# Row transposes of the first three tiles, of the sample tokens and of the memory keys and values: on TensorE instead of by DMA

## The chip, the cores and the metric

One Trainium2 chip, all 8 cores, each with its own eighth of the prompt streams and of the sample streams; the cores don't exchange data. The time is that of the slowest core, in microseconds of the device, as the median of several runs. One execution was profiled as well; its trace is of the slowest of its cores, core 2, unless another is named.

## The reference, cut to what matters

One layer for two groups of tokens with shared weights. Cut to shapes and order:

```
z = x @ w_in                       # 1024 -> 2560: u | v | B | C | x_in
a = u * (W_s masked @ layernorm(v) + b_s)          # per 128-token block, 4 heads
b = B * conv3(C * x_in)                            # causal, depthwise
x = layernorm(ALPHA * x + [a | b] @ w_out)
q = x @ w_q ; p = softmax(q . mem_k / 16) ; o = p @ mem_v    # 256 memory tokens, 4 heads
x = layernorm(ALPHA * x + o @ w_mem_o)
x = layernorm(ALPHA * x + (silu(x @ w_gate) * (x @ w_up)) @ w_down)   # 1024 -> 2816 -> 1024
```

The prompt group has 8 streams of 8192 frames and its memory keys and values come from `mem_prompt @ w_mem_k` and `@ w_mem_v`, which are outputs too; the sample group has 16 streams of 32 frames with cached keys and values. A core gets one prompt stream (16 tiles of 512 tokens) and two sample streams (64 tokens).

## The kernel before

Matmuls take bf16 operands and want the contracted dimension on the partitions. Activations therefore exist twice: as rows (token on the partition, f32, `xbuf` for a tile, `xS` for the sample), where the residual and the layer norm are computed, and as features (`F0`, `F2` for a tile, `FS0`, `FS2` for the sample, bf16), which the next matmuls read. After the first and after the second layer norm rows must become features. `to_feature` (L553) does this: ACT casts 128 rows of 1024 to bf16 into one of three buffers `xb` (L556), and a DMA transpose issued from ACT's queue writes them into the feature tile (L557). A prompt tile has four such row blocks for each of the two norms, the sample one of 64 rows for each.

Memory keys and values of the prompt are made by `mem_proj` (L804): eight blocks of 128 x 512 (`mk` and `mv`, two halves, two blocks of 128 memory tokens). VectorE copies a block to `sg` (L811), SP stores it to the output (L812), ACT casts it to `kst` (L816) and a DMA transpose of L817 puts it into `KT` or `VT`, which share the memory of `F2` and so appear as `F` in the trace (`kst` appears as `hS` or `hT`). `fold_m` multiplies `KT` with `w_q`, `fold_n` multiplies `VT` with `w_mem_o`, so that later tiles need one matmul each for scores and output (L797 to L801 evacuate them).

A tile has a part A (projections, convolution, two layer norms: `in_proj_v`, `in_proj_c`, `out_half`, `scores`, again `out_half`) and a part B (`gate_up`, `down`, third layer norm, store). Part B of tile t runs beside part A of tile t + 1. The start is different: part A of tile 0, part A of tile 1 up to the first norm, the sample and the memory work all share the first pass over the weights (`first_A`); `rest_A` finishes tile 1 beside part B of tile 0, and the second transposes of tile 1 stand at the end of that pass (`to_tile(c1, s, 1)`, priority 1.2, last lines of `build`).

Weights lie in HBM as f32 pieces (`w_pieces`). GpSimd's queue loads a piece with a cast to bf16 (L461) into a ring of three slots (A) or four (B); SP stores cast pieces once to scratch (`wsc`, L448) and later loads come from there (L457). The A pieces are cast again for tile 2 and stored then, the B pieces are stored for tile 0 or 1, so from tile 3 on nothing is cast but the inputs `x_prompt_t` (L484).

All instructions are first collected with their reads, writes, an estimated duration and a priority (`Sched.op`), then a list scheduler (`order`) plays them through a simple model of engines and DMA rings and fixes the order of each engine's queue; `emit` adds the semaphore waits. Each engine executes its queue strictly in that order. PSUM has eight banks, four in pool "A" (`in_proj`, `out_half`, `scores`, sample), four in pool "B" (`gate_up`, `down`, memory), each handed out round robin in program order (`bank`). All matmuls have the line of one helper, L422; a layer norm is L540 and L542 (residual and statistics), L545, L517, L519 on GpSimd, L548 and L550.

Of the kernel before, what the change touches and what calls it, by code (L numbers as in the profile page):

```python
# [7 lines left out]
F32 = mybir.dt.float32  # L8
BF16 = mybir.dt.bfloat16
AF = mybir.ActivationFunctionType  # L10
ALU = mybir.AluOpType
# [5 lines left out]
EPS = 1e-5  # L17
NCORES = 8
TT = 512
OFF = 0.3  # L20

COMPUTE = ("tensor", "vector", "scalar", "gpsimd")
# [39 lines left out]
class Sched:  # L62
# [12 lines left out]
    def op(self, eng, fn, reads=(), writes=(), dma=None, dur=0.1, nbytes=0, table=None, dprio=0.0):  # L75
        o = Op(eng, fn, dma, dur, self.prio + dprio, nbytes, len(self.ops), table)
        deps = []
        for b in reads:
            deps.extend(b.writers)
            if b.excl:  # L80
                deps.extend(r for r in b.readers if r.eng != eng)
        for b in writes:
            deps.extend(b.writers)
            deps.extend(b.readers)
        seen = set()
        for d in deps:
            if d is o or id(d) in seen:
                continue
            seen.add(id(d))
            o.deps.append(d)  # L90
        for b in reads:
            b.readers.append(o)
        for b in writes:
            if b.readers:
                b.writers = [o]
                b.readers = []
            else:
                b.writers.append(o)
        self.ops.append(o)
        return o  # L100
# [194 lines left out]
def build(NT, debug=False):  # L295
# [38 lines left out]
    with contextlib.ExitStack() as st:  # L334
        def T(name, shape, dt):
            return st.enter_context(nc.sbuf_tensor(name, shape, dt))

        S = Sched(nc)
        op = S.op
        B = {}  # L340

        def buf(name, excl=False):
            if name not in B:
                B[name] = Buf(name, excl)
            return B[name]
# [10 lines left out]
        xb = [T("xb%d" % i, [128, D], BF16) for i in range(NXB)]  # L356
# [9 lines left out]
        biasT = T("biasT", [128, 4, 128], F32)  # L366
        biasS = T("biasS", [128, 4, 32], F32)
        ones_bf = T("ones_bf", [128, 128], BF16)
        WT = T("WT", [128, 4, 128], BF16)
        WTS = T("WTS", [64, 4, 64], BF16)  # L370
        smallT = T("smallT", [128, 36], F32)
        halo_p = T("halo_p", [128, 4, 2], F32)
        mhalf = T("mhalf", [128, 4], F32)
        NST = 11
        stat = [T("stat%d" % i, [128, 4, 6], F32) for i in range(NST)]
        mv = [T("mv%d" % i, [128, 4, 2], F32) for i in range(NST)]
        ve = [T("ve%d" % i, [128, 4], F32) for i in range(NST)]
        rs = [T("rs%d" % i, [128, 4], F32) for i in range(NST)]
# [1 line left out]
        xS = T("xS", [64, D], F32)  # L380
# [11 lines left out]
        def bank(p):  # L392
            i = pool[p][pctr[p] % 4]
            pctr[p] += 1
            return banks[i], b_bank[i]
# [14 lines left out]
        def A(fn, reads, writes, cols, **k):  # L410
            return op("scalar", fn, reads, writes, dur=c_a(cols), **k)

        def P(fn, reads, writes, dur, **k):
            return op("gpsimd", fn, reads, writes, dur=dur, **k)
# [55 lines left out]
        S.prio = -2.0  # L470
        P(lambda e: e.memset(ones_bf[:], 1.0), [], [buf("ones")], 0.3)
        P(lambda e: e.memset(mhalf[:], -0.5), [], [buf("mhalf")], 0.3)
        P(lambda e: e.memset(halo_p[:], 0.0), [], [buf("halo_p")], 0.3)
        P(lambda e: e.memset(WTS[:], 0.0), [], [buf("WTS")], 0.3)
        op("sync", lambda e: e.dma_start(out=smallT[:], in_=small), [], [buf("small")], dma="c0", nbytes=1 << 14)
# [26 lines left out]
        bk, bb = bank("A")  # L502
        MM([(bk[:], sg[1][:, 0:128], tmp[0][:], True, True)], [buf("sg1"), buf("tmp0")], [bb], 2048)
        for h in range(4):
            V(lambda e, h=h, bk=bk: e.scalar_tensor_tensor(
                out=biasT[:, h, :], in0=bk[:, h * 128:(h + 1) * 128], scalar=smallT[:, 4 + h:5 + h],
                in1=sg[0][:, h * 128:(h + 1) * 128], op0=ALU.mult, op1=ALU.add), [bb, buf("small"), buf("sg0")], [buf("biasT")], 128)
        bk, bb = bank("A")
# [41 lines left out]
            V(lambda e: e.scalar_tensor_tensor(out=xv, in0=xv, scalar=rs[i][0:SP, 0:1], in1=lnb[li][0:SP, :],  # L550
                                               op0=ALU.mult, op1=ALU.add), bx + [buf("rs%d" % i), buf("lnb%d" % li)], bx, 1024)

        def to_feature(xv, bx, SP, dst, b_dst):  # L553

            j = rot("xb", NXB)
            A(lambda e: e.activation(out=xb[j][0:SP, :], in_=xv, func=AF.Copy), bx, [buf("xb%d" % j)], 1024)  # L556
            op("scalar", lambda e: e.dma_start_transpose(out=dst, in_=xb[j][0:SP, :]), [buf("xb%d" % j)], [b_dst],  # L557
               dma="tr%d" % j, nbytes=1 << 19)

        class Tile:  # L560
            pass
# [107 lines left out]
        def out_half(c, half, rg, brg, li):  # L669

            if c.sample:
                if half == 0:
                    c.st = 10
                bk, bb = bank("A")
                src, b_src = ((FS1, [buf("FS1_%d" % k) for k in range(8)]), (FSq, [buf("FSq0"), buf("FSq1")]))[li]
                MM([(bk[0:64, :], src[:, k, :], rg[:, k * 512:(k + 1) * 512], k == 0, k == 7) for k in range(8)], b_src + [brg], [bb], 512)
                resid(bk, bb, xS[:], [buf("xS0"), buf("xS1")], half, 64, c.st)
                if half == 1:
                    ln_apply(xS[:], [buf("xS0"), buf("xS1")], 64, li, c.st)
                    d_, b_ = ((FS0, "FS0"), (FS2, "FS2"))[li]  # L680
                    to_feature(xS[:], [buf("xS0"), buf("xS1")], 64, d_[:], buf(b_))
                return
            for s in range(4):
                bk, bb = bank("A")
                MM([(bk[:], c.F1[:, k, s * 128:(s + 1) * 128], rg[:, k * 512:(k + 1) * 512], k == 0, k == 7) for k in range(8)],
                   [buf(c.pre + "F1_%d" % k) for k in range(8)] + [brg], [bb], 512)
                i = s
                bx = c.bx[s]
                resid(bk, bb, c.x[s], bx, half, 128, i)
                if half == 1:  # L690
                    ln_apply(c.x[s], bx[:1], 128, li, i)
                    if not c.hold:
                        to_tile(c, s, li)

        def to_tile(c, s, li):
            d_, b_ = ((F0, "F0_%d"), (F2, "F2_%d"))[li]
            to_feature(c.x[s], c.bx[s][:1], 128, d_[:, :, s * 128:(s + 1) * 128], buf(b_ % s))

        def scores(c, hp, rg, brg):

# [102 lines left out]
        def mem_proj(pn, half, dsto, dT, b_dT):  # L803

            rg, brg = piece("B", "%s%d" % (pn, half), 0, 0.0)
            for mc in range(2):
                bk, bb = bank("B")
                MM([(bk[:], memT[:, k, mc * 128:(mc + 1) * 128], rg[:, k * 512:(k + 1) * 512], k == 0, k == 7) for k in range(8)],
                   [buf("memT"), brg], [bb], 512)
                j = rot("sg", 2)  # L810
                V(lambda e, bk=bk, j=j: e.tensor_copy(out=sg[j][:], in_=bk[:]), [bb], [buf("sg%d" % j)], 512)  # L811
                op("sync", lambda e, j=j, mc=mc: e.dma_start(  # L812
                    out=dsto[mc * 128:(mc + 1) * 128, half * 512:(half + 1) * 512], in_=sg[j][:]), [buf("sg%d" % j)], [],
                   dma="o_kv%d" % j, nbytes=1 << 18)
                i = rot("kst", 3)
                A(lambda e, bk=bk, i=i: e.activation(out=kst[i], in_=bk[:], func=AF.Copy), [bb], [buf("kst%d" % i)], 512)  # L816
                op("scalar", lambda e, i=i, mc=mc: e.dma_start_transpose(  # L817
                    out=dT[:, half * 4:half * 4 + 4, mc * 128:(mc + 1) * 128], in_=kst[i]), [buf("kst%d" % i)], [b_dT],
                   dma="tk%d" % i, nbytes=1 << 18)

        def fold_m(hp):
            rg, brg = piece("B", "qT%d" % hp, 0, 0.0)
# [315 lines left out]
```

How the kernel before makes its waits and increments, by code:

```python
                def body(eng, ops=ops, e=e):  # L256
                    waited = {}
                    dwaited = {}
                    for o in ops:
                        for pe_, d in o.best.items():
                            if waited.get(pe_, 0) < d.sig:
                                eng.wait_ge(sems[pe_], d.sig)
                                waited[pe_] = d.sig
                        for s, c in o.dmadeps.items():
                            if dwaited.get(s, 0) < c:
                                eng.wait_ge(dsems[s], c)
                                dwaited[s] = c
                        inst = o.fn(eng)
                        if o.dma:
                            inst.then_inc(dsems[o.stream], 16)
                        elif o.signal:
                            inst.then_inc(sems[e], 1)
                    if e == final_wait_eng:
                        for s, c in total.items():
                            if dwaited.get(s, 0) < c:
                                eng.wait_ge(dsems[s], c)
```

## Time and profile before

| what | us |
|---|---|
| median of 3 runs (lowest, highest) | 3443.89 (3429.8, 3456.57) |
| profiled execution | 3434.8 |
| its span on the slowest core (fastest core) | 3433.2 (3377.1) |
| TensorE busy, share of the span | 3189.5, 93% |
| VectorE / ACT / GpSimd busy | 50% / 27% / 11% |

A span runs from the first to the last instruction of a core; the execution's time is that of the slowest core with what lies around it. Busy time of TensorE counts matmuls in flight, not its peak. Waits and releasers are worked out from semaphores. `ACTq` is ACT's queue issuing a DMA, and share of DMA is the mean over the core's 16 DMA engines, where q0 is the software queue (loads issued by GpSimd), q1 the one of SP and q10 that of ACT's transposes.

### The profile page before, as it was taken

To read this page: it belongs to the slowest core of one execution; us is meant where nothing else is said; L and a number is where in the kernel's file an instruction comes from. 1 tells how busy PE (TensorE), PEld (TensorE's weight loads), DVE (VectorE), ACT (ScalarE), POOL (GpSimd) and SP (SyncE) were. 2 spreads that over 40 slices of the span, in tenths; PEclk is the share of its full clock that TensorE was granted. 3 is DMA by queue.
4 is the path that set the end of the run, shared out by engine and by line. 5 is a ranking of instruction groups with operands and counts; after the bars stand their busy time and mean duration, and the time that the engine had idled before them with its cause. 6 is when DMAs were issued, how large, how long until landed. Compare 5 with 4: busy or idle time off the path is not lost.

```text
span 3433.2 us, 45794 instructions; the slowest of 8 cores (3377.1 to 3433.2 us)
## 1 busy us (share of the span) xinstructions
PE 3189.5 (93%) x15332; PEld 1453.7 (42%) x15332; DVE 1707.4 (50%) x3148; ACT 912.8 (27%) x1463; POOL 382.3 (11%) x345
## 2 busy tenths in 40 slices
PE   7755979668999999999999999999999999999997
PEld 3322434233444444444444444444444444444443
DVE  4453324344464565545464565545464555545453
ACT  3132111122423314142423214142423224142410
POOL 2011101010010111011010111011010111111010
PEclk9877989889999999999999999999999999999999
DMA  9878899997655565656565565566565665666453
GB/s 176 161 141 114 165 123 224 183 189 187 173 180 198 167 219 170 205 173 213 169 189 189 175 213 177 197 178 208 172 190 191 172 220 166 207 176 207 137 179 107
DMA packets 232917, 616.17 MB, mean 179 GB/s; under 512 B 150832, under 2 KB 150960, under 8 KB 174704
## 3 DMA queue, kind: packets, MB, share of 16 engines
q1 hardware_dynamic: 81136, 505.35, 44.1%
q0 software_dynamic: 10944, 73.03, 13.5%
q10 hardware_dynamic: 140608, 34.88, 8.9%
q8 instruction: 127, 2.08, 0.2%
q14 instruction: 102, 0.84, 0.1%
HBM read 586.47 MB, written 64.89 MB: 190 GB/s over the span
## 4 chain that ended last, share of the span: by engine, by line
PE 86%; DMA 8%; ACTq 2%; issue 1%; DVE 1%; ACT 1%; POOL 0%; POOLq 0%; DVEq 0%; SPq 0%
PE bank L422 86%; DMA F<-xb 4%; ACTq L557 2%; DMA F<-hS 1%; DMA y_prompt<-xbuf 1%; DMA xbuf<-x_prompt 1%; DMA rb<-w_pieces 1%; POOL rs L519 0%; DMA ra<-w_pieces 0%; DMA hT<-x_prompt_t 0%; DVE xbuf L550 0%; ACT xb L556 0%; DVE stat L542 0%; ACT vh L598 0%; DVE xbuf L540 0%
## 5 line engine op out<-in xcount | busy, mean ns | idle before, releaser
L422 PE MATMUL bank<-F,rb 128*128 128x512 bf16 (+1 forms) x5696 | 1257.7, 380 | 84.9 <-DMA F<-xb 36.3
L422 PEld LDWEIGHTS bank<-F,rb 128*128 128x128 bf16 x5696 | 558.9, 98 | 759.3 <-issue 102.0
L422 PE MATMUL bank<-F,ra 128*128 128x512 bf16 x2944 | 676.5, 383 | 89.7 <-ACT vh L598 60.7
L422 PE MATMUL bank<-rb,hT 128*128 128x512 bf16 (+1 forms) x2832 | 628.1, 380 | 0.0
L744 DVE TENSOR_TENSOR hT<-bank,sg 128x512 bf16<-128x512 f32 x352 | 240.9, 688 | 749.6 <-PE bank L422 632.4
L519 POOL TENSOR_TENSOR rs<-ve,mhalf 128x1 f32<-128x1 f32 (+3 forms) x260 | 339.6, 1308 | 2202.2 <-DVE ve L517 2069.6
L422 PE MATMUL bank<-ra,F 128*128 128x512 bf16 x2400 | 534.2, 381 | 9.5 <-DVE xbuf L540 5.9
L422 PEld LDWEIGHTS bank<-F,ra 128*128 128x128 bf16 x2944 | 287.4, 99 | 434.2 <-issue 107.0
L422 PEld LDWEIGHTS bank<-rb,hT 128*128 128x128 bf16 (+1 forms) x2832 | 276.4, 98 | 333.7 <-issue 5.2
L743 ACT ACTIVATE sg<-bank 128x512 f32<-128x512 f32 x352 | 209.7, 596 | 759.0 <-PE bank L422 691.6
L540 DVE SCALAR_TENSOR_TENSOR xbuf<-xbuf,bank 128x512 f32<-128x512 f32 x384 | 256.2, 671 | 222.3 <-PE bank L422 214.1
L422 PEld LDWEIGHTS bank<-ra,F 128*128 128x128 bf16 x2400 | 235.4, 98 | 295.6 <-issue 15.1
L556 ACT ACTIVATE xb<-xbuf 128x1024 bf16<-128x1024 f32 x128 | 135.2, 1057 | 703.1 <-DVE mv L545 543.5
L542 DVE BATCH_NORM_STATS2 stat<-xbuf 128x6 f32<-128x512 f32 x384 | 263.3, 690 | 18.7 <-DVE xbuf L540 0.5
L550 DVE SCALAR_TENSOR_TENSOR xbuf<-xbuf,rs,lnb 128x1024 f32<-128x1024 f32 x192 | 244.6, 1275 | 4.3 <-POOL rs L519 3.7
L548 DVE SCALAR_TENSOR_TENSOR xbuf<-xbuf,mv,lng 128x1024 f32<-128x1024 f32 x192 | 244.7, 1275 | 0.0
L718 DVE TENSOR_TENSOR F<-F,rden 128x512 bf16<-128x512 bf16 x128 | 82.8, 688 | 207.2 <-ACT rden L716 183.5
L637 DVE TENSOR_TENSOR cx<-bank,xin 128x512 f32<-128x512 f32 (+1 forms) x68 | 44.2, 651 | 247.6 <-PE bank L422 246.7
L646 DVE SCALAR_TENSOR_TENSOR acc<-cx,smallT,acc 128x512 f32<-128x512 f32 (+1 forms) x136 | 97.8, 719 | 74.6 <-ACT acc L644 71.5
L598 ACT ACTIVATE vh<-bank,nm,rs 128x128 bf16<-128x128 f32 x240 | 106.5, 456 | 100.3 <-DVE nm L532 41.4
L630 ACT ACTIVATE xin<-bank 128x512 f32<-128x512 f32 (+1 forms) x68 | 39.0, 574 | 295.9 <-PE bank L422 295.9
L743 ACT ACT_TABLE_LOAD x69 | 88.5, 1283 | 69.3 <-PE bank L422 67.4
(103 smaller groups left out, 1072.0 us busy)
## 6 DMA issues: line engine op xcount, KB each, us to landing
rb<-wsc SPq DMA_DIRECT2D x216, 1024.0 KB, 5.9
ra<-wsc SPq DMA_DIRECT2D x147, 1024.0 KB, 5.7
rb<-w_pieces POOLq DMA_DIRECT2D x34, 1024.0 KB, 16.2
xbuf<-x_prompt SPq DMA_DIRECT2D x16, 2048.0 KB, 8.9
y_prompt<-xbuf SPq DMA_DIRECT2D x64, 512.0 KB, 5.7
rb<-wsc SPq DMA_DIRECT2D x28, 768.0 KB, 5.6
wsc<-rb SPq DMA_DIRECT2D x16, 1024.0 KB, 14.3
F<-x_prompt_t POOLq DMA_DIRECT2D x15, 1024.0 KB, 10.0
```

Source lines behind the costliest of these rows:

```text
L422: i_ = e.matmul(o_, lhsT=l_, rhs=r_, start=s_, stop=p_)
L519: P(lambda e: e.tensor_tensor(out=rs[i][0:SP, 0:n], in0=ve[i][0:SP, 0:n], in1=mhalf[0:SP, 0:n], op=ALU.pow), [buf("ve%d" % i), buf("mhalf" ...
L540: V(lambda e: e.scalar_tensor_tensor(out=xv[:, sl], in0=xv[:, sl], scalar=ALPHA, in1=bk[0:SP, :], op0=ALU.mult, op1=ALU.add), [bb, bx[half ...
L542: V(lambda e: e.bn_stats(out=stat[i][0:SP, half, :], in_=xv[:, sl]), [bx[half]], [buf("stat%d" % i)], 512)
L548: V(lambda e: e.scalar_tensor_tensor(out=xv, in0=xv, scalar=mv[i][0:SP, 0, 0:1], in1=lng[li][0:SP, :], op0=ALU.subtract, op1=ALU.mult), bx ...
L550: V(lambda e: e.scalar_tensor_tensor(out=xv, in0=xv, scalar=rs[i][0:SP, 0:1], in1=lnb[li][0:SP, :], op0=ALU.mult, op1=ALU.add), bx + [buf( ...
L556: A(lambda e: e.activation(out=xb[j][0:SP, :], in_=xv, func=AF.Copy), bx, [buf("xb%d" % j)], 1024)
L598: A(lambda e: e.activation(out=c.vh[:, s, h * 128:(h + 1) * 128], in_=bk[:, h * 128:(h + 1) * 128], func=AF.Identity, scale=rs[i][:, h:h + ...
L646: V(lambda e, k=k: e.scalar_tensor_tensor(out=ac3, in0=cx3[:, :, k:k + L], scalar=smallT[:, w0 + k:w0 + k + 1], in1=ac3, op0=ALU.mult, op1 ...
L718: V(lambda e, mc=mc: e.tensor_tensor(out=FT[:, 2 * h + mc, :], in0=FT[:, 2 * h + mc, :], in1=rden[:, 0:n], op=ALU.mult), [buf("rden"), buf ...
L743: A(lambda e, bg=bg, i=i: e.activation(out=sg[i][:], in_=bg[:], func=AF.Silu), [bbg], [buf("sg%d" % i)], 512, table="silu")
L744: V(lambda e, bu=bu, i=i, f=f: e.tensor_tensor(out=hT[:, f, :], in0=bu[:], in1=sg[i][:], op=ALU.mult), [bbu, buf("sg%d" % i)], [buf("hT%d" ...
```

## The change

An identity matrix `ident` is made by GpSimd at the start. A new function `flip` transposes n blocks of 128 columns on TensorE into one PSUM bank (read as bf16) and has ACT copy the bank to the feature tile. `to_feature` calls it where `on_pe` is set: for the sample rows always, for a prompt tile where `c.t < T_DMA`, that is for tiles 0, 1 and 2; from tile 3 on the DMA transpose stays. `mem_proj` calls it always. The rows' flips take a bank of pool "A", those of the memory one of pool "B". To make room for `ident`, most `stat` tiles shrink.

```diff
+T_DMA = 3
+        ident = T("ident", [128, 128], BF16)
-        stat = [T("stat%d" % i, [128, 4, 6], F32) for i in range(NST)]
+        stat = [T("stat%d" % i, [128, 4 if i in (8, 9) else 2, 6], F32) for i in range(NST)]
...
+        P(lambda e: e.memset(ident[:], 0.0), [], [buf("ident")], 0.3)
+        P(lambda e: e.affine_select(out=ident[:], in_=ident[:], compare_op=ALU.not_equal, fill=1.0, base=0,
+                                    pattern=[[-1, 128]], channel_multiplier=1), [buf("ident")], [buf("ident")], 0.5)
...
-        def to_feature(xv, bx, SP, dst, b_dst):
+        def flip(src, b_src, SP, n, dst, b_dst, pl):
+
+            bk, bb = bank(pl)
+            pv = bk[:].bitcast(BF16)
+            W = SP if SP < 128 else 128
+
+            def fn(e):
+                for c in range(n):
+                    i_ = e.transpose(pv[:, c * W:(c + 1) * W], src[:, c * 128:(c + 1) * 128], ident[0:SP, 0:SP])
+                return i_
+            op("tensor", fn, [b_src, buf("ident")], [bb], dur=0.07 * n)
+            A(lambda e: e.activation(out=dst, in_=pv[:, 0:n * W].rearrange("p (c i) -> p c i", c=n), func=AF.Copy), [bb], [b_dst], n * W)
+
+        def to_feature(xv, bx, SP, dst, b_dst, on_pe):
 
             j = rot("xb", NXB)
             A(lambda e: e.activation(out=xb[j][0:SP, :], in_=xv, func=AF.Copy), bx, [buf("xb%d" % j)], 1024)
-            op("scalar", lambda e: e.dma_start_transpose(out=dst, in_=xb[j][0:SP, :]), [buf("xb%d" % j)], [b_dst],
-               dma="tr%d" % j, nbytes=1 << 19)
+            if on_pe:
+                flip(xb[j][0:SP, :], buf("xb%d" % j), SP, 8, dst, b_dst, "A")
+            else:
+                op("scalar", lambda e: e.dma_start_transpose(out=dst, in_=xb[j][0:SP, :]), [buf("xb%d" % j)], [b_dst],
+                   dma="tr%d" % j, nbytes=1 << 19)
...
-                    to_feature(xS[:], [buf("xS0"), buf("xS1")], 64, d_[:], buf(b_))
+                    to_feature(xS[:], [buf("xS0"), buf("xS1")], 64, d_[:], buf(b_), True)
...
-            to_feature(c.x[s], c.bx[s][:1], 128, d_[:, :, s * 128:(s + 1) * 128], buf(b_ % s))
+            to_feature(c.x[s], c.bx[s][:1], 128, d_[:, :, s * 128:(s + 1) * 128], buf(b_ % s), c.t < T_DMA)
...
-                op("scalar", lambda e, i=i, mc=mc: e.dma_start_transpose(
-                    out=dT[:, half * 4:half * 4 + 4, mc * 128:(mc + 1) * 128], in_=kst[i]), [buf("kst%d" % i)], [b_dT],
-                   dma="tk%d" % i, nbytes=1 << 18)
+                flip(kst[i], buf("kst%d" % i), 128, 4, dT[:, half * 4:half * 4 + 4, mc * 128:(mc + 1) * 128], b_dT, "B")
```

## Rows read from the trace of the kernel before

**Rows 1.** The page, TensorE's granted clock in 40 slices, tenths of full speed.

```profile
PEclk9877989889999999999999999999999999999999
```

**Rows 2.** Stretch 800 to 3400 us: length, busy (instructions) per engine, clock, DMA, GB/s.

```profile
800.00:3400.00 2600.00, 2599.99 (x12198) 1184.44 (x12197) 1373.02 (x2478) 744.14 (x1144) 283.57 (x220) 1.00 0.60 187
```

**Rows 3.** TensorE's waits, core 2: releaser, us in total, times, longest.

```profile
PE bank L422 <- DMA F<-xb: 62.5, 2, 36.3
PE bank L422 <- ACT vh L598: 60.7, 2, 37.6
PE bank L422 <- DMA F<-hS: 24.1, 2, 23.3
PE bank L422 <- ACT sg L743: 20.1, 3, 11.9
...
PE bank L422 <- DMA rb<-w_pieces: 5.4, 1, 5.4
```

**Rows 4.** ACT in order of time, 640 to 670 us: start, length, instruction.

```profile
649.72 17.41 ACTq L557 DMA_TRANSPOSE F<-xb  x1
667.28 1.09 ACT L743 ACTIVATE sg<-bank 128x512 f32<-128x512 f32 x2 [17.04 <-issue]
```

**Rows 5.** DMA issues, 0 to 780 us and 1000 to 3400: count, us to landing.

```profile
F<-xb ACTq DMA_TRANSPOSE x24, 21.4
...
F<-xb ACTq DMA_TRANSPOSE x96, 4.3
```

**Rows 6.** A stretch of 5 us in the wait that ends at 342.

```profile
310.00:315.00 5.00, 0.00 (x0) 0.00 (x0) 0.43 (x1) 0.00 (x0) 0.00 (x0) 0.50 1.40 18
```

**Rows 7.** DMA queues, 0 to 780 us: packets, MB, share of 16 engines.

```profile
q0 software_dynamic: 9216, 60.44, 51.2%
q1 hardware_dynamic: 11192, 58.83, 23.6%
```

**Rows 8.** DMA queues, 0 to 130 us.

```profile
q0 software_dynamic: 2612, 14.99, 76.7%
q1 hardware_dynamic: 2962, 8.81, 23.2%
```

**Rows 9.** Spans of two cores.

```profile
core 2: 3433.2 us, clock 0.965
core 3: 3418.9 us, clock 0.968
```

**Rows 10.** TensorE's waits on core 3.

```profile
PE bank L422 <- ACT vh L598: 69.2, 3, 34.0
PE bank L422 <- DMA F<-xb: 58.7, 2, 54.3
PE bank L422 <- DMA F<-hS: 19.7, 2, 18.4
...
PE bank L422 <- ACT sg L743: 5.6, 3, 2.4
```

**Rows 11.** TensorE in order of time, 783 to 870 us.

```profile
783.69 9.17 PE L422 MATMUL bank<-F,ra 128*128 128x512 bf16 x32 [37.56 <-ACT vh L598]
...
794.43 0.39 PE L422 MATMUL bank<-WT,vh 128*128 128x128 bf16 x4
794.65 12.25 PE L422 MATMUL bank<-rb,hT 128*128 128x512 bf16 x56
...
860.93 7.07 PE L422 MATMUL bank<-ra,F 128*128 128x512 bf16 x32
```

**Rows 12.** Groups by shape, TensorE, 1000 to 3000 us: busy, mean ns of one.

```profile
L422 PE MATMUL bank<-WT,vh 128*128 128x128 bf16 x172 | 16.6, 219 | 0.0
```

**Rows 13.** Chain that ended last, 715 to 735 us: start, length, piece.

```profile
722.06 0.70 DVE xbuf L540
...
728.88 37.06 DMA F<-xb
```

**Rows 14.** Stretch 342 to 452 us, columns as in rows 2.

```profile
342.00:452.00 110.00, 104.57 (x767) 52.43 (x767) 38.57 (x64) 20.19 (x37) 11.20 (x16) 0.94 0.85 174
```

**Rows 15.** GpSimd in order of time, first microseconds.

```profile
1.07 0.20 POOL L471 MEMSET ones_bf<- 128x128 bf16 x1 [0.36 <-POOLq L296]
```

## The prediction

> **What bounds the kernel now.** I read the slices of the span first. TensorE's granted clock stands at 9 tenths or more from the tenth slice on and falls to 8 and 7 in slices before it [rows 1]. One row of the stretches says the rest: from 800 to 3400 us the matmuls fill 2599.99 of 2600 us at clock 1.00 [rows 2]. Nothing in this change can shorten that part. It holds the same instructions before and after, and what the change could still do to it is to disturb it. The gain can only come from the first 800 us, and from there only by TensorE's idle time, its low clock, or less work.
>
> Next, TensorE's waits. Four releasers carry most of its idle time, all of it before 800 us: ACT L598 60.7 us, the landing of `F<-xb` 62.5, the landing of `F<-hS` 24.1, ACT L743 20.1; together 167.4 us, in seven long waits and two short ones [rows 3]. `F<-xb` and `F<-hS` are the DMA transposes of L557 and L817. The two ACT lines are the same thing at one remove: in ACT's order of time the transpose issue of L557 at 649.72 holds ACT's queue for 17.41 us, and the Silu of L743 behind it starts at 667.28 [rows 4]. So ACT, which should drain PSUM, stands behind an issue that cannot be passed on. A weight load shows up for 5.4 us only [rows 3].
>
> Why are these transposes slow? The same 128x1024 transpose takes 21.4 us (median, 24 of them) from issue to landing in the first 780 us and 4.3 us (96 of them) in the steady part [rows 5]. While one is due, the queues hardly move: 18 GB/s from 310 to 315 us [rows 6], against 187 GB/s in the steady part [rows 2]. The difference between the two parts is the traffic of the software queue q0, the casting weight loads: 51.2% of 780 us here [rows 7]. Whatever the mechanism, a transpose among casting loads costs four to five times as much as one without, and the engines are idle in part of it.
>
> By the Trainium skill, page "Advanced Engine Details and Errata", section "X-Bar Transpose (TRN2)", transpose DMAs are as fast as regular ones; the trace fits it in the steady part (4.3 us) and not in the start (21.4 us). By that rule a transpose would land late only because the DMA engines are full, which is the first rival below.
>
> **The change, part by part.** Removed: 24 transposes of L557 for tiles 0 to 2 (both layer norms, four rows each), 2 for the sample rows, 8 of L817. All 34 lie before 800 us, so those of tile 3 and later, which stay, meet the steady 4.3 us.
>
> 1. The waits go: -167.4 us on core 2. Is that true of the slowest core afterwards? Core 3 has 69.2 + 58.7 + 19.7 + 5.6 = 153.2 us of the same four, and 3418.9 - 153.2 = 3265.7; core 2 gives 3433.2 - 167.4 = 3265.8 [rows 9, 10]. So the cores end level and core 2 may stand for all. (A few us of ACT L598 and L743 are not the transposes'; I leave them in, since the issues on ACT also cause part of smaller waits that I don't count.)
>
> 2. The clock comes back. After a long wait 32 matmuls take 9.17 us instead of 7.07 [rows 11]: 2.1 us, seven times, -15 us.
>
> 3. TensorE now transposes: 26 x 8 + 8 x 4 = 240 of 128x128. The trace has no such operation. The nearest is the 128x128 matmul with a changing stationary tile: four of them start at 794.43 and the next group at 794.65, so 0.055 us each [rows 11]; one alone lasts 0.219 us [rows 12]. Back to back as eight in one group they are nearest to the first: 240 x 0.055 = +13 us; the upper bound is 240 x 0.219 = 53. By the Trainium skill, page "TensorE: Matmul & The Clock Gate", section "Part 4: PE-mode transpose", one costs about 275 ns in a kernel; by that the term would be 66 us, an estimate. No run here shows it yet.
>
> 4. ACT's work stays even: the issue goes, and a PSUM read of 128x1024 comes, which two 128x512 reads price at 1.09 us [rows 4]. ACT is busy 20.19 us of 110 where the weights stream [rows 14], so its idle time takes it: 0. If that cover were gone, 30 reads (26 and 8 of half the size) are 33 us.
>
> 5. What is left of each wait. A flip in TensorE's queue waits for the cast `xb`, and the cast for the layer norm of its row: from the residual of L540 at 722.06 to the transpose's issue at 728.88 is 6.8 us [rows 13]. It is mostly hidden: the wait of 37.6 us that ends at 783.69 [rows 3, 11] began at 746.1, 17 us after that issue, so TensorE had matmuls for longer than the chain. There are eight groups of flips (six of four rows, two of the sample); with one and a half chains left in the open I take 10 us; 0 if all is hidden, 8 x 6.8 = 54 if each group waits for a whole chain.
>
> 6. Weights. DMA work does not shrink with the time: q0 and q1 hold 51.2 + 23.6% of 780 us = 583 us, of which 130 us lie before 130 us, where the two together fill the engines already [rows 7, 8]. The remaining 453 us must now fit into some 510 us, share 0.89. From 342 to 452 us the engines ran at 0.85 with no transpose, the matmuls filled 104.57 of 110 us [rows 14], and the one wait for a load was 5.4 us [rows 3]. About 400 us of the new stretch are like that: 400/110 x 5.4 = 20, less the 5.4 that is in the time now: +14 us. Lower bound 0; the upper one is the first rival.
>
> 7. On POOL a memset and an `affine_select` for `ident` stand before the first weight load: a 128x128 memset is 0.20 us [rows 15]; the other I bound by 0.1 and 1.5: +1 us. The smaller `stat` tiles change nothing.
>
> Sum: 3433.2 - 167.4 - 15 + 13 + 10 + 14 + 1 = 3288.8 us of span. The profiled execution took 1.6 us more than its span, and the median of the runs is 9.1 us above it: 3299 us.
>
> **The rivals.**
> *The DMA engines take over.* For it: 453 us of queue work in a shorter stretch. Against it: the stretch from 342 to 452 us, where loads at 0.85 cost TensorE only 5.4 us [rows 3, 14]. At the share 0.85 the 453 us take 533, the part ends at 130 + 533 = 663 instead of 783, a gain of 120; at the 0.75 that both queues reached over the first 780 us [rows 7], 604 and a gain of 49. With 0.80: 566 us, gain 87, 3357 us.
> *Flips block TensorE's queue.* It is in order; a flip placed too early holds up ready matmuls. Whole chains for all eight groups: 54 instead of 10 us, 3343. For it: the PSUM banks of pool "A" now also hold flips, so a late flip keeps a bank too. Against it: the 17 us of term 5.
> *Dear transposes.* At 0.219 us each, each begun only when the one before is out, +40 us: 3339. For it: nothing that the trace shows; against it: the 0.055 us of four in a row [rows 11]. By the figure of the Trainium skill's TensorE page (term 3) it would be 3352, an estimate.
> *Slower than before.* The same queue, row by row: if each of the 26 rows' flips made TensorE wait for its own chain, 26 x 6.8 = 177 us would replace 10, 3299 + 167 = 3466. It decides from (145 gained + 10) / 26 = 6 us a row, nearly the whole chain each time. Against it: between the rows of one group there are other matmuls (the feed-forward part of the tile before), and only the first tile has few.
> *The change doesn't reach the waits* would need some other wait that ends just after each transpose; that could only be a load, so it is a part of the first rival.
>
> **How the numbers follow.** The forecast has a chance of 0.63 with a range of its own of 3262 to 3323 (all costs at nothing; terms 5 and 6 at twice what I took). DMA 0.15, blocked queue 0.12, dear transposes 0.06, slower 0.04. Predicted is the likeliest, 3299. The range reaches down to all costs at nothing, 3444 - 167 - 15 = 3262, and 5 lower for the smaller waits I didn't count, 3257, and up to 3362, past the named times of the three middle cases: what is left out is the slow case, the upper half of the DMA case and small tails, under 0.2. About 1% is what a measurement of this kernel can tell from no change. Faster by over 1% (under 3409): all but the last case and the DMA case's tail, 0.93; within 1% 0.04; slower 0.03.
>
> **What would show it.** Right: no TensorE wait on `F<-xb` or `F<-hS`, none on ACT L598 above a few us, matmuls without a gap from near 640 us on instead of 783. Term 3 is right if eight transposes take about 0.44 us. Wrong: waits on `rb<-w_pieces` or `ra<-w_pieces` of over 30 us in sum (DMA), or on ACT L556 at a transpose of over 30 us (queue), or a core whose start stays near 783 us.

## The result and the profile after

| what | us |
|---|---|
| changed kernel, 4 runs | 3284.89, 3288.11, 3357.91, 3817.87 (median 3323.01) |
| kernel before, 4 runs | 3429.8, 3443.89, 3456.57, 3993.14 (median 3450.23) |
| ratio after / before, 95% interval | 0.9544 [0.9456, 0.9633] |
| profiled execution after, its span on the slowest core (core 0) | 3288.11, 3286.6 |
| spans of the eight cores after | 3260.5 to 3286.6, mean 3272.9 |
| the same of before (profiled execution) | 3377.1 to 3433.2, mean 3411.3 |

In the two longest runs after, cores 4 to 7 ran at a lower clock (0.96 and 0.84, against 0.99), and these two, the longest run before and such runs everywhere below are left out, so that the kernel's own time is 3285 to 3288 us. On a second chip, where both kernels ran again beside most of the experiments (five runs before, four after), the kernel after took 3278 to 3282 us and the ratio was 0.9506 [0.9486, 0.9526].

The page of the kernel after, core 0: busy tenths of TensorE, its granted clock and the DMA share in 40 slices. The line of the clock answers to [rows 1].

```profile
PE   6788899999999999999999999999999999999997
...
PEclk9899999999999999999999999999999999999999
DMA  9777979965655656565565656556565655655452
```

Of the first ten slices six stood at 8 or 7 before; now one does. The stretches of core 0 (columns as in [rows 2]; the last answers to [rows 14]):

```profile
640.00:3253.00 2613.00, 2613.00 (x12263) 1190.91 (x12262) 1381.07 (x2499) 750.48 (x1160) 285.82 (x222) 1.00 0.59 188
470.00:640.00 170.00, 164.85 (x809) 75.98 (x808) 90.03 (x164) 54.41 (x77) 23.27 (x26) 0.98 0.99 233
342.00:452.00 110.00, 107.14 (x671) 51.66 (x670) 26.24 (x64) 20.21 (x39) 8.92 (x14) 0.98 0.79 149
```

From 640 us on there is no idle TensorE, where before it was near 783. The 170 us ahead of that run at a DMA share of 0.99, and the matmuls still fill 164.85 of them.

TensorE's waits after, core 0 (releaser: us in total, times, longest), to be held against [rows 3]. L837 is the cast `kst` of the memory blocks, L574 the cast `xb`, L569 the copy of a flip out of PSUM, L619 and L764 are L598 and L743 of before:

```profile
PE bank L566 <- ACT hT L837: 14.6, 1, 14.6
PE bank L424 <- DMA rb<-w_pieces: 10.5, 3, 6.2
PE bank L424 <- DMA ra<-w_pieces: 7.1, 1, 7.1
PE bank L566 <- ACT xb L574: 6.1, 5, 3.2
...
PE bank L424 <- ACT F L569: 4.8, 5, 1.3
...
PE bank L566 <- ACT hS L837: 2.9, 1, 2.9
...
PE bank L424 <- ACT sg L764: 1.0, 2, 0.8
...
PE bank L424 <- ACT vh L619: 0.3, 1, 0.3
```

The four waits of the sum, 167.4 us, are down to 1.3, and `F<-xb` and `F<-hS` are not in the list at all. All rows of the list add up to 77.6 us, against 225.9 before (core 2): 148.3 us less. The span of the slowest core is 146.6 us shorter. With 13 us of new transposes, about 11 us are left over for the clock: 146.6 - 148.3 + 13. These are two different cores; core 2 alone, whose waits fell to 59.6 us and whose span fell by 172.7, leaves 19: 172.7 - 166.3 + 13.

What came in is the first row. It follows from a store. The chain that ended last, 100 to 175 us (start, length, piece):

```profile
121.74 0.70 DVE sg L832
122.47 0.03 issue
122.50 29.03 DMA mem_k_prompt<-sg
...
151.62 0.70 DVE sg L832
152.36 0.04 issue
152.41 0.60 ACT hS L837
153.01 0.14 issue
153.15 0.59 PE bank L566 x4
```

A block's output store of 256 KB takes 29.03 us to land, VectorE's next copy into `sg` (two buffers) waits for it, the cast `kst` stands behind that copy in program order, and the flip, in TensorE's strict order, waits for the cast. Before, what stood behind that cast was a DMA, not an instruction of TensorE.

### The profile page after: what moved, and what is told of

Same layout as the page of the kernel before. It is cut to its first block, busy times and chain, and to the rows that moved or that the text cites. A ratio compares the mean times of both kernels' runs of the same rounds, so it can differ in the third digit from the quotient of the medians.

```text
span 3286.6 us, 46253 instructions; the slowest of 8 cores (3260.5 to 3286.6 us)
## 1 busy us (share of the span) xinstructions
PE 3191.1 (97%) x15572; PEld 1465.2 (45%) x15572; DVE 1708.5 (52%) x3148; ACT 946.3 (29%) x1501; POOL 383.9 (12%) x347
## 3 DMA queue, kind: packets, MB, share of 16 engines
q1 hardware_dynamic: 81136, 505.35, 45.4%
## 4 chain that ended last, share of the span: by engine, by line
PE 92%; DMA 4%; issue 1%; DVE 1%; POOL 0%; ACT 0%; POOLq 0%; DVEq 0%; ACTq 0%; SPq 0%
PE bank L424 92%; DMA rb<-w_pieces 1%; DMA mem_k_prompt<-sg 1%; DMA y_prompt<-xbuf 1%; DMA xbuf<-x_prompt 1%; DMA F<-x_prompt_t 1%; PE bank L566 0%; POOL rs L524 0%; DMA vh<-mem_k_t 0%; DVE stat L531 0%; DVE xbuf L555 0%; DVE mv L534 0%; ACT F L569 0%; DVE xbuf L545 0%; DVE ve L522 0%
## 5 line engine op out<-in xcount | busy, mean ns | idle before, releaser
L424 PE MATMUL bank<-F,ra 128*128 128x512 bf16 x2944 | 669.6, 380 | 3.0 <-ACT F L569 1.8
L764 ACT ACTIVATE sg<-bank 128x512 f32<-128x512 f32 x352 | 209.8, 596 | 729.7 <-PE bank L424 671.8
L574 ACT ACTIVATE xb<-xbuf 128x1024 bf16<-128x1024 f32 x128 | 135.3, 1057 | 607.7 <-DVE mv L550 508.2
L619 ACT ACTIVATE vh<-bank,nm,rs 128x128 bf16<-128x128 f32 x240 | 106.4, 456 | 81.2 <-DVE nm L537 63.8
## 6 DMA issues: line engine op xcount, KB each, us to landing
wsc<-rb SPq DMA_DIRECT2D x16, 1024.0 KB, 15.1
```

Source lines behind the costliest of these rows:

```text
L424: i_ = e.matmul(o_, lhsT=l_, rhs=r_, start=s_, stop=p_)
L619: A(lambda e: e.activation(out=c.vh[:, s, h * 128:(h + 1) * 128], in_=bk[:, h * 128:(h + 1) * 128], func=AF.Identity, scale=rs[i][:, h:h + ...
L764: A(lambda e, bg=bg, i=i: e.activation(out=sg[i][:], in_=bg[:], func=AF.Silu), [bbg], [buf("sg%d" % i)], 512, table="silu")
```

## The experiments

The theory: DMA transposes are slow because casting loads (the software queue q0) run beside them; moved to TensorE, the waits go and each transpose costs 0.055 us. The rivals that remained: full DMA engines as such, ACT's queue alone, the software queue whether it casts or not, and a price of flips hidden by luck.

Times in "us" are of the slowest core. Since one late core decides these, I also compare the mean span of the eight cores, by which executions of one kernel agree better. On the chip of the experiments that mean is 3425.9 for the kernel before (six runs, 3412.8 to 3433.4) and 3268.4 for the changed kernel (four runs, 3267.8 to 3269.2): the change is worth 157.5 us there, on the mean core. The last experiment, e11, ran on another chip, where the kernel before had 3425.1. Most experiments rest on one execution of eight cores. e4 and e11 leave rows untransposed: they keep the traffic and compute something else.

| run | what | us | mean of cores | against after |
|---|---|---|---|---|
| e1 | memory blocks alone on TensorE | 3418.67 | 3394.4 | +126 |
| e2 | rows and sample alone on TensorE | 3303.58 | 3292.2 | +23.8 |
| e3 | all 16 tiles on TensorE | 3329.91 | 3318.3 | +49.9 |
| e4 | plain copies in place of transposes | 3330.64 | 3316.7 | +48.3 |
| e5 | before, transposes issued by SP | 3380.8 | 3353.1 | +84.7 |
| e6 | casts in tiles 3 to 5 too | 3376.21 | 3314.4 | +46.0 |
| e7 | e6, those tiles on TensorE | 3289.53 | 3281.0 | +12.6 |
| e10 | tiles 3 to 5 by software queue, no cast | 3281.36 | 3272.2 | +3.8 |
| e11 | e6, plain copies in those tiles | 3274.68 | 3265.6 | -2.8 |
| e8 | `kst` ahead of the `sg` copy | 3281.02 | 3266.8 | -1.6 |
| e9 | `kst` first and four staging buffers | 3271.11 to 3275.11 | 3262.9 | -5.5 |

### The parts one by one: e1 and e2

e1 (against the changed kernel):

```diff
-T_DMA = 3
+T_DMA = 0
-                    to_feature(xS[:], [buf("xS0"), buf("xS1")], 64, d_[:], buf(b_), True)
+                    to_feature(xS[:], [buf("xS0"), buf("xS1")], 64, d_[:], buf(b_), False)
```

> The change with only the eight memory blocks on TensorE; rows of tiles and sample by DMA as before. Theory (each wait is its own transposes' price, so parts add up): the 24 us of F<-hS go and little else, span about 3405 to 3415 against 3433 before; TensorE still waits some 140 us on F<-xb, ACT L598 and ACT L743. Rival (engines are full, fewer transposes only shift the load): the waits on F<-xb grow by about what is saved, span above 3425.

Measured: 3418.67, with the kernel before at 3461.27 beside it. The time lies between the two expected bands, nearer the theory's; the bands were set from the execution of 3434.8, so the difference on one chip is the better measure: 31.5 us on the mean core. The waits on the rows' transposes are as before (core 2, to be held against [rows 3]):

```profile
PE bank L424 <- DMA F<-xb: 66.1, 3, 35.5
PE bank L424 <- ACT vh L619: 62.8, 2, 46.2
...
PE bank L566 <- ACT hT L837: 9.3, 1, 9.3
```

The wait on `F<-hS` is gone, that of the flips on `kst` is there. L764 has 0.9 us on this core, but up to 23.9 on others, so it still belongs to the rows.

e2 puts the DMA transpose of before back into `mem_proj` in place of `flip(kst[i], ...)` and keeps the rest.

> The change with the rows of tiles 0 to 2 and of the sample on TensorE, memory blocks by DMA. Theory: the F<-hS wait of some 24 us stays, everything else of the gain comes, span about 3300 to 3315 (3287 of the change plus 24, less the 15 us that the changed kernel still loses in front of the memory blocks). Rival (parts not additive): below 3290 or above 3340.

Measured: 3303.58, as the theory had it: 133.7 us on the mean core. What is left is the memory's own wait (core 7):

```profile
PE bank L424 <- DMA F<-hS: 21.9, 1, 21.9
```

31.5 + 133.7 = 165.2 against 157.5 for both: within the scatter of before's means the two parts add up, and neither needs the other.

### The price on TensorE: e3

`T_DMA = 16`: the transposes of tiles 3 to 15, 13 x 2 x 4 x 8 = 832 of 128x128, go to TensorE as well.

> All sixteen tiles on TensorE. Theory: from tile 3 on the DMA transposes cost TensorE nothing, since it is never idle there, so 104 more groups of eight at 0.44 us each are pure cost: 3287 + 46 = 3333 us, range 3325 to 3345. Rival: the later DMA transposes slow the loads or ACT in a hidden way, and taking them out gives some of it back: 3320 or less.

Measured: 3329.91. The mean core is 49.9 us longer than after on the same chip (45.4 against the first profiled execution): 0.055 to 0.060 us each. TensorE in order of time shows it, in e3 and alike in the changed kernel. These three lines are e3's, core 3 (start, length, instruction):

```profile
1009.77 0.61 PE L566 MATMUL bank<-ident,xb 128*128 128x128 bf16 x8
1010.22 3.62 PE L424 MATMUL bank<-rb,hT 128*128 128x512 bf16 x16
1013.67 0.61 PE L566 MATMUL bank<-ident,xb 128*128 128x128 bf16 x8
```

and these of the kernel after, core 0:

```profile
544.62 0.61 PE L566 MATMUL bank<-ident,xb 128*128 128x128 bf16 x8
545.07 3.19 PE L424 MATMUL bank<-F,rb 128*128 128x512 bf16 x14
```

The whole group of the kernel after, core 0 (duration in ns, min/median/max; first and last start in us):

```profile
L566 PE MATMUL bank<-ident,xb x208: 186/219/314, 166.5 to 635.3; 128*128 128x128 bf16 x96, 64*128 64x64 bf16 x8
```

A single one is in flight for 219 ns (median), but the next matmul starts 0.45 us after eight of them: they overlap, as the matmuls with changing weights did in [rows 11]. The run says two things more. From tile 3 on a DMA transpose costs TensorE nothing, so the threshold in the change is on the right side. And 104 more reads of eight flips each cost ACT nothing that TensorE waits for: e3 has no TensorE wait after 640 us.

### Transpose or any DMA in that place: e4, and the queue: e5

e4 (against the changed kernel; the sample rows stay on TensorE):

```diff
-            if on_pe:
+            if on_pe and SP == 128:
+                op("scalar", lambda e: e.dma_start(out=dst, in_=xb[j].rearrange("p (c i) -> p c i", c=8)), [buf("xb%d" % j)], [b_dst],
+                   dma="tr%d" % j, nbytes=1 << 19)
+            elif on_pe:
...
-                flip(kst[i], buf("kst%d" % i), 128, 4, dT[:, half * 4:half * 4 + 4, mc * 128:(mc + 1) * 128], b_dT, "B")
+                op("scalar", lambda e, i=i, mc=mc: e.dma_start(
+                    out=dT[:, half * 4:half * 4 + 4, mc * 128:(mc + 1) * 128],
+                    in_=kst[i].rearrange("p (c i) -> p c i", c=4)), [buf("kst%d" % i)], [b_dT],
+                   dma="tk%d" % i, nbytes=1 << 18)
```

> As the changed kernel, but the rows of tiles 0 to 2 and the memory blocks are moved by a plain DMA copy of the same bytes from SBUF to SBUF on ACT's queue, in pieces of 256 bytes, and not transposed (the features of these tiles are left untransposed); the sample rows are transposed on TensorE. It asks whether it is the transpose or any transfer at that place that lands late. Theory (the transpose itself is slow beside casting loads): copies land in 5 to 10 us, ACT's queue is not held, TensorE's waits on them are under 50 us in sum, span 3290 to 3340. Rival (the DMA engines are full, so anything lands late there): copies land in about 20 us like the transposes, waits over 120 us, span 3400 or more.

Measured: 3330.64, inside the theory's band, but with more wait than it had allowed (50.9 us on `F<-xb` and 17.8 on `F<-hS`), landings a little over its 5 to 10 us, and single issues that were held for up to 13.9 us. The copies of the rows, core 6 (issue on ACT's queue in ns, min/median/max; landing in us; who waited):

```profile
L576 ACTq DMA_DIRECT2D F<-xb x24: 601/602/13924, 170.9 to 678.8; - x24
...
  ACT xb L574: 56.7, 4
  PE bank L424: 50.9, 3
...
DMA to landing us min/median/max: 2.9/10.7/31.2
```

The same question to the kernel before, its first 780 us, core 2:

```profile
L557 ACTq DMA_TRANSPOSE F<-xb x24: 1248/1922/26683, 179.4 to 767.2; - x24
...
DMA to landing us min/median/max: 3.0/19.4/50.3
```

(That is the median of all 26 issues of the line, the sample's two among them; [rows 5] has the 24 of the tiles.) By the mean of the cores, 48 of the 157 us stay with plain copies in that place. That fits the rival of full engines for this part, but no run takes the fill away there, so it is not shown. The other 109 us, about two thirds, are the difference between transposing and copying by DMA.

e5 (against the kernel before) issues both kinds of transposes from SP: `op("scalar", ...)` becomes `op("sync", ...)` at L557 and L817, nothing else.

> The kernel before, with every DMA transpose issued by SP's queue instead of ACT's; nothing else is edited (the order of the queues follows from it). It separates the two ways in which a slow transpose costs: its landing, and the queue that stands behind its issue. Theory: both are real, so the waits on ACT L598 and L743 (80 us on core 2 before) go nearly wholly, the waits on F<-xb and F<-hS (87 us) stay, and part of the gain comes back as weight loads from scratch that stand behind the issues on SP: span 3350 to 3400. Rival: the ACT waits were the landing in disguise, and what TensorE would do next needs the transposed rows anyway: span 3415 or more, with F<-xb waits grown by 50 us or more.

Measured: 3380.8, 72.8 us less on the mean core, with the transposes where they were. Core 2:

```profile
PE bank L422 <- DMA F<-xb: 72.4, 3, 31.4
PE bank L422 <- DVE xbuf L540: 25.6, 2, 21.6
PE bank L422 <- ACT vh L598: 22.2, 3, 12.5
```

ACT L598 falls from 60.7 to 22.2 and L743 to 0.9, as they would if ACT stood behind its own issues [rows 4]. `F<-xb` itself stays. `F<-hS`, which I had expected to stay, is not in the list (at most 3.2 us on any core), and a wait on L540 comes in. So nearly half of the gain could be had by moving the issue alone, and the other half did not come that way. The longest wait on L540, 21.6 us, ends behind a copy into `sg` on VectorE (L811, at 157.00 us) that itself waited 19.20 us for a store of `mem_k_prompt`: the same chain of stores that the changed kernel meets at its flips.

### Is it the cast? e6, e7, e10, e11

These four bring the traffic of the start into the steady part, where nothing else is odd: no first pass over the weights, no memory work, TensorE never idle. In e6 `STORE_AT` of the A pieces is 6 instead of 2, so that tiles 3 to 5 load them from f32 with a cast, while their rows are transposed by DMA. e7 adds `T_DMA = 7`. e10 loads the same pieces in tiles 3 to 5 by the same software queue, but in bf16 from scratch:

```diff
-            if name in stored:
+            if name in stored and r == "A" and 3 <= t < 6:
+                src = wsc[sidx[name]]
+                op("gpsimd", lambda e: e.dma_start(out=dst[:, 0:nco], in_=src[:, 0:nco]), [buf("wsc_" + name)], [b],
+                   dma="g%s%d" % (r, i), nbytes=256 * nco, dprio=dprio)
+            elif name in stored:
```

e11 keeps e6's casts and moves the rows of tiles 3 to 5 by the plain copy of e4.

> The changed kernel (DMA transposes from tile 3 on), but the seven A pieces are loaded with a cast from f32 in tiles 3 to 5 too and stored only in tile 6, so that casting loads meet DMA transposes in tiles 3 to 5. Theory (transposes are slow beside casting loads): the 24 transposes of these tiles land in 10 us or more instead of 4 to 5, and TensorE waits 20 to 100 us in the stretch of 640 to 1250 us where it waits not at all now: span 3305 to 3390. Rival (the first 640 us are slow for another reason, the sheer fill of the engines): landings stay under 7 us, waits under 10, span below 3300.

> As the run with casts up to tile 5, but rows of tiles 0 to 6 are transposed on TensorE. It is the control for it: the same casting loads with no DMA transpose beside them. Theory: only the price of 4 x 8 more groups of eight transposes, 32 x 0.44 = 14 us: 3287 + 14 = 3301, range 3294 to 3312, no wait over 5 us after 640 us. Rival (the casting loads themselves are what holds TensorE up): waits on ra<-w_pieces of over 20 us after 640 us, span above 3320.

> The changed kernel, but in tiles 3 to 5 the A pieces are loaded from scratch (bf16, no cast) by GpSimd's software queue instead of by SP. It asks what of the casting loads disturbs the transposes: the cast from f32 or the software queue. If the cast (twice the bytes read, 2-byte elements written): the 24 transposes of these tiles land in 4 to 5 us and TensorE does not wait after 640 us, span 3280 to 3292. If the software queue: landings of 7 us or more in the median with single ones over 20, waits of 15 us or more on most cores, span 3300 or more.

> As the run with casts up to tile 5 (tiles 0 to 2 on TensorE, casting loads in tiles 3 to 5), but the rows of tiles 3 to 5 are moved by plain DMA copies on ACT's queue instead of DMA transposes; these rows are left untransposed. It is the last corner of the square: casting loads beside a transfer that is no transpose, with engines that are not full. Theory (it takes a transpose and a cast together): copies land in 3 to 7 us, no single one over 20, ACT's issues stay under 1 us, no wait of TensorE over 5 us after 640 us, span 3275 to 3292. Rival (any transfer between casts is late): single landings over 20 us, waits of 15 us or more on most cores, span 3300 or more.

Rows of tiles 3 to 5, 640 to 1260 us: issue time on ACT's queue and landing, in order e6 (cores 7 and 4), e10 (core 3), e11 (core 6). e6, its slowest core first:

```profile
L578 ACTq DMA_TRANSPOSE F<-xb x23: 1232/1317/16872, 729.7 to 1249.3; - x23
...
DMA to landing us min/median/max: 3.0/7.1/59.9
```

```profile
L578 ACTq DMA_TRANSPOSE F<-xb x24: 1247/1250/4737, 720.4 to 1200.3; - x24
...
DMA to landing us min/median/max: 3.1/6.8/38.8
```

e10:

```profile
L582 ACTq DMA_TRANSPOSE F<-xb x24: 1232/1234/1573, 727.9 to 1202.5; - x24
...
DMA to landing us min/median/max: 3.1/5.1/7.2
```

e11:

```profile
L578 ACTq DMA_DIRECT2D F<-xb x24: 601/602/1853, 716.9 to 1193.2; - x24
...
DMA to landing us min/median/max: 2.9/4.1/28.8
```

Transposes beside casting loads cost 46.0 us on the mean core and 95 on the slowest. Take the DMA transposes away (e7: 256 more flips at 0.055 us are 14 us, and 12.6 were measured), the cast away (e10: 3.8) or make a plain copy of the transpose (e11: 2.8 less), and the cost is gone. After 640 us no core of e7 and e10 has a TensorE wait and none of e11 over 1.5 us; in e6 every core has one, from 5.2 us (core 4) to 85.6 (core 7). For the time it takes both: the software queue by itself doesn't do it (e10), nor do casting loads beside a plain copy (e11). e10 also carries less, since the cast reads f32: the core read 586.5 MB from HBM against 615.8 in e6, and q0 held 16.9% of those 620 us against 26.7%. Whether the conversion counts or the larger load is therefore not told apart. The spans of e7, e10 and e11 (3287.9, 3279.8, 3273.1) lie below their bands, which start from the 3287 us of the first chip.

The landings say it less sharply. e6's medians are 6.0 to 8.1 us over the cores, below the 10 and more that I had expected, with single ones of 35 to 60 us. But e11's copies, too, have single landings of 23 to 29 us on six of the eight cores, where I had expected none over 20, with medians of 4.0 to 7.0; only e10 has none over 7.7. So casting loads make a copy late as well now and then. What e11 lacks is the held issue: 4.1 us at most, against up to 20 in e6 in this window. In e6, 93% of the wait after 640 us is on ACT L619, behind ACT's queue, and core 4, with a landing of 38.8 us but no issue over 4.7, waits only 5.2 us. In this stretch the damage goes through the issue that holds ACT's queue, and hardly through a landing that TensorE itself waits for (2.2 us, on one core).

e6 also shows one of them at work. ACT and TensorE in order of time, core 7:

```profile
1267.45 29.63 ACTq L578 DMA_TRANSPOSE F<-xb  x1
1297.29 4.11 ACT L619 ACTIVATE vh<-bank,nm,rs 128x128 bf16<-128x128 f32 x8 [29.91 <-issue]
...
1299.65 4.75 PE L424 MATMUL bank<-F,ra 128*128 128x512 bf16 x11 [44.03 <-ACT vh L619]
```

It is [rows 4] again: the issue holds ACT's queue for 29.63 us, the activation behind it is late, TensorE waits 44.03 us. The DMA queues from 1280 to 1295 us (packets, MB, time that their packets took as a share of 16 engines):

```profile
q10 hardware_dynamic: 539, 0.13, 116.5%
q0 software_dynamic: 19, 0.14, 21.4%
```

and of the kernel before from 310 to 315 us, the stretch of [rows 6]:

```profile
q10 hardware_dynamic: 91, 0.02, 92.2%
q0 software_dynamic: 9, 0.07, 48.1%
```

Most of the recorded time there belongs to the packets of the transposes: 1.165 x 16 x 15 / 539 = 0.52 us for a packet of 256 bytes in e6, and 0.81 us before. A sum of over 100% says that the times of one engine's packets overlap, so that they can hold waiting, and the trace doesn't tell waiting from moving. These two windows also lie inside long waits. Over whole stretches a packet took 0.163 x 16 x 780 / 29254 = 0.070 us before (first 780 us, core 2), and 0.061 x 16 x 620 / 25344 = 0.024 us in the steady part of the kernel after (640 to 1260 us, core 0):

```profile
q10 hardware_dynamic: 29254, 7.23, 16.3%
...
q10 hardware_dynamic: 25344, 6.29, 6.1%
```

In the same way e6 has 0.065 us and e10 0.031. The packets of plain copies have 0.018, in the first 780 us of e4 as beside the casts of e11: it is the transposes' packets that stretch. Of the 91% that the three queues held in the first 780 us before, the transposes made 16.3. Why their packets take longer while casting packets are in flight, the runs don't show.

### The new wait: e8 and e9

e8 moves the cast to `kst` ahead of VectorE's copy to `sg` in `mem_proj`, two lines moved up.

> The changed kernel, with the cast to kst of a memory block put ahead of the copy to sg, so that a flip no longer stands behind the store of an earlier block. Theory (the wait of 14.6 + 2.9 us on ACT L837 on core 0, 0 to 12 us on the others, is the store of 256 KB that lands 29 us late): it goes, mean span of the cores 3273 - 8 = 3265, slowest core 3270 to 3278. Rival: TensorE runs into the next wait there (weights qT, rows of tile 0) and nothing is gained: mean 3270 or more.

Measured: 3281.02, 1.6 us less on the mean core, in one execution too little to tell from nothing. The wait on L837 went, and the same wait came back as the bank's: 4.4 us on the mean of the cores, as L837 has in the changed kernel on that chip. Core 3:

```profile
PE bank L424 <- DVE sg L834: 14.1, 3, 7.4
```

VectorE still waits for the store, and the PSUM bank is free only when VectorE has read it. The wait went as the theory had it, and nothing was gained, as the rival had it. e9 therefore also stages the blocks in four buffers, halves of `lng2` and `lnb2`, whose gains are loaded after the last memory block instead of before:

```diff
-                j = rot("sg", 2)
-                V(lambda e, bk=bk, j=j: e.tensor_copy(out=sg[j][:], in_=bk[:]), [bb], [buf("sg%d" % j)], 512)
+                j = rot("stg", 4)
+                sv = (lng, lnb)[j // 2][2][:, (j % 2) * 512:(j % 2 + 1) * 512]
+                V(lambda e, bk=bk, sv=sv: e.tensor_copy(out=sv, in_=bk[:]), [bb], [buf("stg%d" % j)], 512)
...
+            at(0.62)
+            load_ln(2, [], [buf("stg%d" % q) for q in range(4)])
```

> The changed kernel with kst cast first, and with the eight f32 memory blocks staged for their stores in the four halves of the third layer norm's gain and offset tiles, which are not needed before 400 us; the loads of those two tiles follow the stores instead of preceding them. No block of the first four waits for a store any more. Theory (what was left of the wait, 14.1 us on VectorE L834 on core 3 and 2 to 6 on others with kst first, was the store's landing at one remove, through VectorE's queue and the PSUM banks): these waits go, mean span of the cores 3262 (3258 to 3266), slowest about 3270, some 0.4% under the changed kernel. Rival (TensorE meets the weights of the memory projections or the first tile's rows there): mean 3266 or more, no difference to kst first.

Measured in three rounds: 3271.11, 3272.63, 3275.11; ratio to before 0.9489 [0.9459, 0.952]. The changed kernel had 3277.71 to 3281.68 beside it, and its best mean core (3267.8) is above e9's worst (3264.2): the gain is 5.5 us on the mean core, about 0.2%, little but apart. No wait on `kst` or the staging copy is left on any core of its profile. The two gain loads move in this run as well, and what that does is not told apart. It is the fastest version that was run.

## Why the prediction held, step by step

- **Bound.** Right. All of the gain came out of the first 800 us; TensorE is without a gap from 640 us on.
- **Term 1, the waits, -167.4.** Right in kind and size: 166 of 167.4 us went. The reason given, transposes among casting loads, is shown by e6, e7, e10 and e11 where it can be isolated, in tiles 3 to 5; there nearly all of the wait came through ACT's held queue. In the start e5 shows that part of it came that way (72.8 of 157.5 us), and e4 that 48 of 157 us stay when the transposes become plain copies, which the prediction had given to transposing as a whole.
- **Term 2, the clock, -15.** About 11 (slowest cores) to 19 (core 2) are left over for it when the waits and the transposes are taken out of the span; the row of slices agrees. No run isolates it.
- **Term 3, 0.055 us a transpose, +13.** Right: 0.45 us for eight, and 0.055 to 0.060 over 832 more in e3. The Trainium skill, page "TensorE: Matmul & The Clock Gate", section "Part 4: PE-mode transpose", has about 275 ns for one in a kernel; the trace differs for the cost in a stream (0.055 to 0.060) and is nearer for one in flight (219 ns median).
- **Term 4, ACT, 0.** Right: 24 reads of 1.02 us each in the list of ACT's groups, and 4.8 us of TensorE's waits on them, which belong to term 5.
- **Term 5, the residue, +10.** Right for the rows: 6.1 on `xb` and 4.8 on the copies, 10.9. But it counted only the eight groups of rows. The eight memory blocks have a chain too, over the `sg` buffers and their stores, and 14.6 + 2.9 = 17.5 us of it stand on core 0 (1.0 to 17.5 over the cores). This is the step that failed. The description of the kernel told how `sg`, SP's store and the cast follow one another, and the prediction didn't ask what the flip, now in TensorE's queue, would wait for there; e9 gets 5.5 us of it back.
- **Term 6, weights, +14.** Over-sized: 10.5 + 7.1 against 5.4 + 7.2 us before, +5. (The prediction named the 5.4 on `rb` as the only wait for a weight load; the full list of core 2 also has 7.2 us on `ra`.) The share came out as foreseen or higher (0.99 from 470 to 640 us), the price didn't: the wait in 110 us at 0.85 was scaled by length, but it was one event and not a rate. The first rival had the right premise and no cost.
- **Term 7, +1.** Not measured apart.
- **Core 2 for all.** It didn't hold. Core 2 fell by 172.7 us to 3260.5, core 0 by 135.4 to 3286.6 and became the slowest, mainly by the memory's wait: 15.1 of the 26.1 us between the two cores. The span of 3286.6 beside the predicted 3288.8 owes part of its closeness to errors that cancel: the weights 9 us too dear, the memory's wait left out, and the slowest core another one.
- **From the span to the median, +9.1.** It didn't carry over: the runs of the kernel after lie within 4 us of one another on either chip, where the three of before spread over 27 us (and its cores over 56 us in one execution, against 26 after). 3299 should have been about 3290.
- **Rivals.** Blocked queue: 10.9 us of rows, not 54, so no. Dear transposes: no, by e3. Row-by-row: no. Full engines: yes for the share, no for the time (+5 us of weight waits).

## What to carry to other kernels

Before a DMA is blamed or moved, put the traffic around it into a stretch where nothing else is odd and take away one thing at a time: here TensorE waited neither for transposes beside uncast loads nor for plain copies beside casting loads, but for the two together, and the transposes in the stretch that casts its weights were cheaper on TensorE. Look at the issue as well as at the landing: a late landing that nobody needs yet costs nothing, an issue that holds the queue of an engine that drains PSUM does. Group the transposes by eight into one PSUM bank and price them at their spacing, not at the time one is in flight. When a DMA becomes an instruction of an in-order engine, follow the chain of its source buffer as far as the stores that free it: what the DMA's queue used to wait out, the engine now waits for.

## What the runs showed of the hardware that I had not expected

- A DMA transpose of 128x1024 beside casting loads landed in 21.4 us in the median in the start and in 6.0 to 8.1 us in e6, with single ones of 35 to 60, against 4.0 to 5.3 and at most 7.7 beside uncast loads (e10). Its packets of 256 bytes took 0.065 to 0.070 us over whole stretches, instead of 0.024 to 0.031. The Trainium skill, page "Advanced Engine Details and Errata", section "X-Bar Transpose (TRN2)", has transpose DMAs as fast as regular ones. Beside casting loads the traces do not agree: e11's plain copies landed in 4.0 to 7.0 us in the median and in 29 at most, and their packets took 0.018 us.
- The issue of such a transpose held ACT's queue for up to 29.63 us, where it takes 1.23 otherwise. That of a plain copy beside casts was held for 4.1 us at most (e11), in the fuller start for up to 13.9 (e4).
- At a DMA share of 0.99 over 170 us TensorE lost only 5 us: there a full share by itself told little about the time.
